# Seven norms of a residual stream applied behind the products instead of ahead of them

## The reference, cut to what matters

```python
def rms_norm(x, g):
    xf = x.astype(jnp.float32)
    return (xf * lax.rsqrt(jnp.mean(xf * xf, axis=-1, keepdims=True) + EPS) * g).astype(x.dtype)

# first block, l = 0, 1                    (norms 0 to 3)
h = rms_norm(x, norm_mix[l])               # norms 0, 2
z = h @ w_in[l]                            # q, k, v, forget logits, convolution, recurrence
...                                        # forgetting attention, short convolution, hgrn2
x = x + y @ w_out[l]
h = rms_norm(x, norm_ffn[l])               # norms 1, 3
x = x + (silu(h @ w_gate) * (h @ w_up)) @ w_down        # l = 0
x = x + moe_swiglu(h, ...)                 # l = 1: router, top 2 of 8 experts

# second block, l = 0, 1                   (norms 4 to 7)
h = _rms_norm(x, ln1_g[l])                 # norms 4, 6
proj = h @ w_in[l]                         # three attentions and their gates
...                                        # axial, differential, latent attention
x = x + merged @ w_out[l]
h2 = _rms_norm(x, ln2_g[l])                # norms 5, 7
x = x + square(relu(h2 @ w_ff1[l])) @ w_ff2[l]
return _rms_norm(x, final_g)               # norm 8
```

## Time and profile before

| | |
|---|---|
| median of 3 runs | 2799.46 us (2795.32 to 2799.68) |
| profiled execution, its span | 2802.39 us, 2800.6 us |
| PE busy | 2589.1 us, 92% |
| DVE busy | 1858.0 us, 66% |
| ACT busy | 1495.3 us, 53% |
| memory read | 581.72 MB, 208 GB/s over the span |
| chain that ended last | PE 83%, DVE 10%, ACT 4% |
| PE waits for ACT's probabilities `pt` (L591) | 36.2 us in 22 waits |
| PE waits for DVE's `hlo` (L877) | 33.5 us in 8 waits |
| PE waits for ACT's squares `hT` (L516) | 24.6 us in 5 waits |
| PE waits for DVE's `qe` (L1026) | 13.7 us in 4 waits |

### The profile page before, as it was taken

One profiled execution on the slowest core, in us unless ns is written; L12 is line 12 of the kernel. 1 busy time (PEld: TensorE's weight loads), 2 busy tenths in 40 slices (PEclk: granted clock), 3 DMA queues, 4 the chain that ended last, 5 costly groups with the idle time before them and its releaser, 6 DMA issues.

```text
span 2800.6 us, 38554 instructions
## 1 busy us (share of the span) xinstructions
PE 2589.1 (92%) x16790; PEld 2307.7 (82%) x16790; DVE 1858.0 (66%) x1586; ACT 1495.3 (53%) x1442; POOL 0.2 (0%) x4
## 2 busy tenths in 40 slices
PE   6879999887899999999999998998899999988998
PEld 6769998776787878787787876887789988878998
DVE  5755445574688888888888886546565554666554
ACT  5244344442577767677777775446444444554443
POOL 0000000000000000000000000000000000000000
PEclk9979999997899999999999998999899999999999
DMA  5214554321399989999899997433245543323452
GB/s 208 91 61 151 181 185 162 106 91 61 147 363 350 366 348 365 347 359 355 346 366 346 367 349 265 148 111 121 76 151 183 190 148 127 106 106 130 157 183 89
DMA packets 83019, 585.32 MB, mean 209 GB/s; under 512 B 9368, under 2 KB 11128, under 8 KB 12192
## 3 DMA queue, kind: packets, MB, share of 16 engines
q1 hardware_dynamic: 82848, 582.81, 55.9%
HBM read 581.72 MB, written 1.05 MB: 208 GB/s over the span
## 4 chain that ended last, share of the span: by engine, by line
PE 83%; DVE 10%; ACT 4%; issue 1%; DMA 0%; ACTq 0%; SPq 0%; DVEq 0%
PE PS L1397 81%; DVE wlo L854 2%; ACT whi L501 1%; ACT pb L577 1%; PE PS L1781 1%; PE PS L1543 1%; DVE hT L871 1%; ACT pt L591 1%; DVE stat L960 1%; DVE pb L968 1%; DVE small L867 1%; DVE pb L954 0%; DVE qe L1026 0%; DVE ke L1025 0%; DVE lf L1013 0%
## 5 line engine op out<-in xcount | busy, mean ns | idle before, releaser
L854 DVE TENSOR_TENSOR wlo<-raw,whi 128x2048 fp32r<-128x2048 f32 x550 | 1259.1, 2291 | 489.4 <-ACT whi L501 478.9
L501 ACT ACTIVATE whi<-raw 128x2048 fp32r<-128x2048 f32 x550 | 1051.8, 1913 | 377.5 <-PE PS L1397 376.5
L1397 PE MATMUL PS<-hhi,whi 128*128 128x256 f32 x1952 | 568.7, 291 | 26.9 <-DVE hlo L877 24.0
L1397 PE MATMUL PS<-hlo,whi 128*128 128x256 f32 x1952 | 560.3, 287 | 0.0
L1397 PE MATMUL PS<-hhi,wlo 128*128 128x256 f32 x1952 | 559.8, 287 | 0.0
L1397 PEld LDWEIGHTS PS<-hhi,whi 128*128 128x128 f32 x1952 | 381.9, 196 | 40.7 <-issue 35.3
L1397 PEld LDWEIGHTS PS<-hlo,whi 128*128 128x128 f32 x1952 | 382.7, 196 | 0.6 <-issue 0.5
L1397 PEld LDWEIGHTS PS<-hhi,wlo 128*128 128x128 f32 x1952 | 382.5, 196 | 0.0
L1397 PE MATMUL PS<-whi,xghi 128*128 128x512 f32 x896 | 360.3, 402 | 2.1 <-ACT pm L680 2.1
L1397 PE MATMUL PS<-whi,xglo 128*128 128x512 f32 x896 | 354.9, 396 | 0.0
L1397 PE MATMUL PS<-wlo,xghi 128*128 128x512 f32 x896 | 354.8, 396 | 0.0
(11 more groups left out here) (330 smaller groups left out, 3657.9 us busy)
## 6 DMA issues: line engine op xcount, KB each, us to landing
raw<-in_wm SPq DMA_DIRECT2D x336, 1024.0 KB, 5.0
raw<-in_ws SPq DMA_DIRECT2D x214, 1024.0 KB, 4.8
xT<-in_xT SPq DMA_DIRECT2D x1, 1024.0 KB, 4.7
bsum<-in_bsum SPq DMA_DIRECT2D x1, 1024.0 KB
out_T<-hT SPq DMA_DIRECT2D x4, 256.0 KB, 2.5
lmask<-in_lmask SPq DMA_DIRECT2D x1, 512.0 KB
tri<-in_tri SPq DMA_DIRECT2D x1, 256.0 KB
cmask<-in_cmask SPq DMA_DIRECT2D x1, 256.0 KB
```

What stands on the lines that cost most here:

```text
L501: act.activation(whi[s % SPLIT][:], raw[s % RAW][:], ACT.Copy).then_inc(hi_ready, 1)
L854: dve.tensor_tensor(wlo[s % SPLIT][:], raw[s % RAW][:], whi[s % SPLIT][:].bitcast(F32), ALU.subtract).then_inc(lo_ready, 1)
L1397: return pe.matmul(out, a, b, start=start, stop=stop, skip_group_check=True)
```

## The change

Norms 0, 1, 2, 4, 5, 6 and 7 no longer scale x ahead of the products. `hhi` and `hlo` are the halves of x times the gain, and the inverse root, one number for each token, multiplies what comes out of the products. Norms 3 (the router reads h) and 8 (the output) still scale first, in `norm`.

- ACT `split_x` (after: L540) writes `hhi` from xT, DVE `split_x` (L939) writes `hlo`, ACT `square` (L533) the squares. DVE adds the squares of the four pairs (`presum`, L946) so that PE needs one of those products instead of eight (`norm_sums`), and two single columns where the root is also wanted by token (`rcol`).
- The root and its inverse (`root`, `inverse`) follow beside the first unit, whose k tiles now come in rounds by pair (`first=True`).
- Results by feature are taken out by DVE times `rstd` (`scaled`, L980), and ACT applies Silu and Tanh afterwards in place. Results by token are taken out by ACT with scale `rcol`. The gated and squared feed-forwards multiply by `rstd` on DVE.
- The forget logits use the halves and are turned afterwards (`forget_turned`).
- The last product of a `down` goes bank by bank and signals each (`bank_done`).

```diff
+            def split_x(i, j):
+                gain = norm_gain(i)
+                x_pair(i, j)
+                for t in (2 * j, 2 * j + 1):
+                    ins = act.activation(hhi[:, t, :], xT[:, t, :], ACT.Copy, scale=gain(t))
+                ins.then_inc(h_hi, 1)
...
+            def project_to_x(i):
                 for j in range(DK // 2):
                     take()
+                    if i == 3:
+                        x_pair(i, j)
+                    else:
+                        split_x(i, j)
+                    square(j)
...
             def first_mixer(l):  # ACT
...
+                out_by_dve()
                 after(flogit_taken)
                 step(act.activation(a, z, ACT.Abs))
                 step(act.activation(e, a, ACT.Exp, scale=-1.0))
                 act.activation(a, e, ACT.Ln, bias=1.0).then_inc(softplus_done, 1)
-                after(f_clipped)
-                act.activation(lf[:], lf[:], ACT.Ln).then_inc(f_logged, 1)
-                act.activation(lf2[:], lf2[:], ACT.Ln).then_inc(f_logged, 1)
-                out_of(7, flat(rq), func=ACT.Silu)
-                out_of(6, flat(ri))
+                act.wait_ge(drained, C.now(drained))
+                act.activation(flat(rq), flat(rq), ACT.Silu)
+                tokens_out(6, ri)
...
+            def inverse(columns):  # DVE
+                if columns:
+                    after(col_rooted)
+                    step(dve.reciprocal(rcol[:, 0:NT], rcol[:, 0:NT]))
+                    dve.tensor_scalar(rcol[:, NT:2 * NT], rcol[:, 0:NT], -1.0, None, ALU.mult).then_inc(cols_ready, 1)
                 after(rooted)
...
+                dve.reciprocal(rstd[:], rstd[:]).then_inc(rstd_ready, 1)
+                after(rstd_ready)
...
+            def split_ahead():
+                return (fillers.pop(0), take()) if fillers else None
+
+            def take_out(filled):
+                if filled and not filled[0].tokens:
+                    f, used = filled
+                    dve.wait_ge(unit_used, used)
+                    scaled(7, f.dst, f.scale).then_inc(drained, 1)
...
             def fill(n=1):
                 for _ in range(min(n, len(fillers))):
-                    f = fillers.pop(0)
-                    drain()
-                    if f.then == "conv":
-                        short_conv(f.layer)
+                    take_out(split_ahead())
...
+            def project_to_x(i):
+                for j in range(DK // 2 + 1):
+                    used = take() if j < DK // 2 else None
+                    if j and i != 3:
+                        split_x(i, j - 1)
+                    if j > 1:
+                        presum(j - 1)
+                    if used:
+                        dve.wait_ge(unit_used, used)
+                        add_to_x(j)
+                presum_out()
...
                 def up(g):  # SwiGLU, DVE
                     i = g % 2
-                    take()
+                    used = take()
+                    if g == 0:
+                        inverse(False)
+                    dve.wait_ge(unit_used, used)
+                    scaled(4 + 2 * i, sil[i][:]).then_inc(gate_scaled, 1)
                     used = take()
                     after(silu_done)
+                    step(dve.tensor_tensor(by_token(sil[i][:]), by_token(sil[i][:]), over_tiles(rstd[:], NT), ALU.mult))
...
-            def norm(i, split=True):  # PE
...
+            def norm_sums(columns):
+                claim(0, 2)
+                after(presummed)
+                ins = mm(PS[:, 0, 0:S], ones[:], hT[:, 0, :], True, True)
+                if columns:
+                    for t in range(NT):
+                        ins = mm(PS[:, 1, t:t + 1], hT[:, 0, t * P:(t + 1) * P], ones[:, 0:1], t == 0, True)
```

More of the change, by code:

```diff
@@ L880, in drain, with presum @@
-            def drain():
-                take()
-                C.next(drained)
+                after(h_hi)
+                for t in (2 * j, 2 * j + 1):
+                    ins = dve.scalar_tensor_tensor(out=hlo[:, t, :], in0=xT[:, t, :], scalar=gain(t),
+                                                   in1=hhi[:, t, :].bitcast(F32), op0=ALU.mult, op1=ALU.subtract)
+                ins.then_inc(h_ready, 1)
+            def presum(j):
+                after(squared, 2 if j == 1 else 1)
+                step(dve.tensor_tensor(pair(hT, 0), pair(hT, 0), pair(hT, j), ALU.add))
@@ L1067, in first_mixer @@
                 levels(0, (0, 1, 2))
-                drain()
+                out_at(6, pair(qkT, 1), used)
+                used = take()
                 levels(0, (3, 4, 5))
-                drain()
+                out_at(7, pair(qkT, 2), used)
+                used = take()
                 levels(0, (6, 7))
@@ L1073, in first_mixer @@
                 step(dve.tensor_copy(kx[:], ke[:, :, LEVELS - 1, :]))
-                drain()
+                out_at(6, pair(qkT, 3), used)
+                take()
                 decayed(1)
@@ L1123, in swiglu @@
                     take()
-                used = take()
-                for j in range(DK // 2):
-                    add_to_x(j, used)
+                sums_to_x(2)
             def router():
@@ L1261, in second_mixer @@
                 for i in range(3):
-                    drain()
+                    used = take()
+                    if i == 0:
+                        inverse(True)
+                    out_at(4 + i % 2, pair(qa, i), used)
                 fillers.extend(waiting_projections2())
@@ L1345, in relu_ffn @@
                     take()
[L1346 to L1348 removed]
+                sums_to_x(6 + 2 * l)
             dve.memset(ones[:], 1.0).then_inc(consts_set, 1)
```

436 lines of the change are left out of this document (265 added, 171 removed).

## The result

The changed kernel took 2812.11 us (median of 11 runs, 2804.75 to 2816.71 without one disturbed run), the kernel before 2799.45 us (11 runs). The ratio is 1.0045, 95% interval 1.0037 to 1.0054: 12.7 us slower, where 8 us faster was forecast. The profiled execution took 2812.11 us, its span 2810.3 us, against 2802.39 and 2800.6.

What follows compares the result with a forecast made beforehand. TensorE's line was taken to bound the kernel nearly everywhere. Terms 36.3 + 1.6 - 4.8 - 17.6 - 2.5 - 5 gave 8.0 us less: 2802.4 to 2794.4 profiled, 2791.5 against the median; overall range 2776 to 2808.

Steps and rivals of the forecast that it cites:

- the ropes weren't covered: Rival: the rope delays are covered, as VectorE's second fill ends early or the rotation is late anyway; 2772 us, 10 in 100.
- the rounds weren't 10 us: Rival: projection rounds of 10 us instead of 7.8 hold back later weights; 16 of 36 us go, 2800 to 2807; 12 in 100.
- the clock cost TensorE: Rival: every new TensorE wait is followed by 6 us at 1.2 GHz, 3 us lost each; 2818 us, 10 in 100.
- behind a table load of 1.28 us the next instruction begins at once: Rival: each ScalarE table switch also drains 1.38 us, costing 14 us more at the fronts; 2805 us, 2 in 100.
- parts 4 and 5: Late rope passes, -17.6 us, and take-outs moved to VectorE, -2.5 us, including 0.6 in two differential-heads rounds per layer.
- part 4: Four ropes: VectorE waits for the second fill's unit before the passes, 3.8 and 5.0 us late, twice each: -17.6 us.
- part 6: TensorE at half clock behind its new waits, beyond what the first-mixer fronts already counted: -5 us (-14 to +3).
- Part 3: Front of the first mixer, twice: lsf stands behind two weight splits and TensorE waits 8.5 us; -4.8 us (-14 to +4).
- part 2: The ends: last norm +1.4, norm 3 -0.5, first attention's convolution moved behind the probabilities +0.7; together +1.6 us (0 to 4).
- the forecast's rounds: Output projection: VectorE's work per pair takes 7.8 us against TensorE's 5.76, putting the last add 6 us behind the last product.
- The norms and the ends: Gaps closed at norms 1, 4, 5, 6, 7, 36.3 us gained; last norm +1.4, norm 3 -0.5.

Runs made afterwards that it cites:

- the ropes mended: Changed kernel with VectorE's rope() splitting the second filler's weights ahead of the three passes and taking that filler out behind them: 2789.6 us, ratio 0.9962.
- the projections mended: Changed kernel with both engines, in the output projections, doing the next unit's weight split before the pieces of x: 2792.0 us, ratio 0.9974.
- +96: Changed kernel with the SBUF arena begun 96 bytes later: 2794.0 us, ratio 0.9982.
- with `lsf`: Changed kernel with VectorE in the first mixer scaling the forget logits early and writing lsf ahead of the second weight split: 2788.6 us, ratio 0.9964.
- all five edits: Changed kernel with rope, lsf and projection reorderings, first weight unit split earlier at the start, and differential heads' take-outs held back a round: 2747.2 us, ratio 0.9810.
- +64: SBUF arena begun 64 bytes later: changed kernel 2795.9 us, ratio 0.9991; with all five edits 2730.4 us, ratio 0.9752.
- +32: SBUF arena begun 32 bytes later: changed kernel 2803.5 us, ratio 1.0014; with all five edits 2733.3 us, ratio 0.9762.
- the three repairs: Changed kernel with one reordering each, in separate runs: ropes' second take-out 2789.6 us, lsf 2788.6 us, projections' weight splits 2792.0 us.
- the new start: Changed kernel with the three repairs and the first weight unit split between the second and third pair of x: 2754.2 us, ratio 0.9835.
- +992: Changed kernel with only the experts' region begun 992 bytes later, its address in the kernel before: 2807.1 us, ratio 1.0024.
- +928: Changed kernel with only the experts' region begun 928 bytes later, its address in the kernel before begun 64 bytes earlier: 2794.8 us, ratio 0.9991.

## Why the prediction was wrong

**The mechanisms were right.** Every wait that it named is there, most at nearly the size named: `lsf` 7.3 and 9.0 us (8.5 forecast), the waits for the ropes' last passes 3.9 and 5.2 us longer than before (3.8 and 5.0), rounds of 7.7 us in the projection ahead of norm 1 (7.8), the norm behind a down product 9.2 (9.4), norm 4 9.9 (10.7), norm 1 6.8 (6.0). In the first unit behind a projection, where two waits of 1.8 us were forecast, TensorE waits 1.9 and 1.3 us at norm 1, once 2.8 at norm 5, 2.6 and 0.8 at norm 7. No rival took place: the ropes weren't covered, the rounds weren't 10 us, the clock cost TensorE 95.4 us of work against 91.8 before, and behind a table load of 1.28 us the next instruction begins at once (the load of 488.83 above, the root at 490.13).

**The step that failed is the sizing of the sum.** The largest term that was mis-sized is the ropes and take-outs of the second mixers (parts 4 and 5): 20.1 us were put, the ledger shows 27.4, and 25.1 in the second profile. Taking out the ropes' part alone gave 22.5 us, where part 4 had put 17.6 and part 6 another 2. The next are the first mixers, and two stretches that were put at nothing. The profiled executions are 17.8 us apart from the forecast:

- Parts 4 and 5, 7.3 in all. "In two rounds that count per layer" was wrong: it was four rounds, 0.6 us each (11.14 against 10.53 us for two rounds), 2.3 us more for both layers. The rest is take-outs elsewhere in the attentions and half clock behind the ropes, not separated, and 2.3 us of it are gone in the second profile (10.0 and 15.1 for 13.5 and 13.9).
- Part 3, 4.1 in all: the fronts lost 7.9 and 0.9 where the first was put at -6.1 and the second at +1.3. The chain to `lsf` came out right: its end lies about 31.7 and 25.2 us behind the first unit's, forecast 31.3 and 24.3. What was too small is the way from there to the take-out of qkT, 7.3 us and at most 8.7 with half clock. It took 10.5 and 10.2 us, since TensorE ran the first 5 to 6 us behind the wait at half clock. In layer 1, behind its wait of 9.0 us (windows view, clock third from the end):

```profile
512.60:514.00 1.40, 1.39 (x7) 1.38 (x8) 0.00 (x0) 0.00 (x0) 0.00 (x0) 0.50 0.57 105
514.00:516.00 2.00, 2.00 (x6) 0.57 (x6) 0.00 (x0) 0.12 (x2) 0.00 (x0) 0.50 0.83 348
516.00:518.00 2.00, 2.00 (x11) 2.00 (x12) 0.47 (x2) 2.00 (x3) 0.00 (x0) 0.57 0.25 102
```

  TensorE's other new wait in layer 0, 7.4 us for the scaled logits ahead of their turn (`hT`, L1175), which VectorE writes only behind the clipping, was not named. It is not where the 4.1 us are: VectorE goes on to the turned logits (L1178, at 48.22) without idle time, so the wait did not delay `lsf`.
- The rests of the first mixers lost 2.4 and 1.0 us, where part 2 had put a gain of 0.7 for the convolution; 4.2 in all. The kernel with the projections mended gets 2.4 and 3.5 us back in these same stretches, whose last splits already stand in the output projection. So the forecast's rounds are in there, and whether the convolution gained anything can't be read.
- SwiGLU and experts, put at nothing, 4.5 us. Both go with the moved buffers: the experts' 3.4 are gone at the old addresses, and the SwiGLU took 190.0 us in every profiled kernel that had its buffers at the change's place, 189.0 in the kernel before, and 186.6 in both that had them at +96.
- Part 6's 5 us for the clock was too much as a term of its own: it is 3.6 net by the measure above, and already lies in the stretches.
- The norms and the ends were 2.7 us short together, norm 7 the most (3.4 for 5.1).

These are 23 less 5, the 17.8 of the profiles. The other 2.9 of the 20.6 us are between profile and median: the profiled execution of the kernel before lay that much above its median, that of the changed kernel on it. The working has small slips too: the pieces of a round add up to 7.9 and not 7.8 us, the chain of part 3 to 15.25 and not 15.0. They change nothing.

**What the removal of a wait is worth** was also undersized: the fixes gave more than their waits, 22.5 us for the ropes with 17.4 of waits gone, 20 us for the projections where their rounds promised 10. In each of these profiles less work is lost to the clock, 86.4 us with the ropes mended, 86.8 with `lsf`, 87.4 with the projections, against 95.4, and 75.2 with all five edits. But the same measure moves by as much with the place of the buffers alone: it is 105.1 us in the changed kernel at +64, and with all five edits 72.3 at +32 and 83.5 at +64. And put into the kernel before, the ropes' wait brought no more of it. So the clock's part of a wait is suggested, not shown, and a fixed price for it fits none of these runs.

## What to carry to other kernels

A take-out that moves to another engine brings its wait with it. Before, that wait was ScalarE's, and nothing that TensorE needed at once stood behind it; on VectorE it stood in front of passes that TensorE waited for. Together with two orders of splits such places cost more (66 us by the three repairs one by one, 58 together with the new start) than the norms gave (33 for the five that the ledger shows by themselves), and each was mended by the order of the instructions alone. When a sum of many terms of both signs comes out near nothing, the range has to hold the sum of their errors, not that of the likeliest case.

Compare two versions of a kernel at equal addresses, or at several. Over the places tried the kernel before took 2793.9 to 2804.2 us and the changed one 2794.0 to 2812.1, so the 12.7 us between them as they stand are no more than what the place of the buffers does.

## What the runs showed of the hardware that was not expected

- With the same instructions, at full clock and without a wait of their own, the products of 128x512 took 396 ns with the experts' region at one address and 390 at another, and those of the feed-forward (`bhi`, 128x256) had means of 282 ns at the change's place and 277 at +64. Moving the arena by 32 to 96 bytes moved the changed kernel from 2812 to 2794 us, and moving it back by 64 bytes moved the kernel before from 2799.5 to 2793.9.
- The effect of a place mostly repeats from kernel to kernel: the experts took 957.4 to 957.8 us in three kernels with their region at +992. At the change's place they took 960.8 to 965.5 in eight, four of them within 0.1 of 960.9. By what rule the address acts stays open: neither 64 bytes nor the distance orders the values in the tables.
- With the faster products the weight loads come into sight. ScalarE waited 0.9 us for them from 780 to 1580 in the kernel before, and 33 to 79 us in the three kernels with the experts at +928, whose TensorE then waited 1.6 to 4.6 us for weights.
